# Output products that begin with branches A and B, a rounded copy of their own for the first block, and the gate stores moved to the front

## The chip, the core and the metric

The kernel runs on one core of one Trainium2 chip. The core has five engines that each work through their own queue of instructions: PE (TensorE, matrix products), DVE (VectorE), ACT (ScalarE), POOL (GpSimd) and SP (SyncE, which only issues transfers here). They meet through semaphores: an instruction can raise one when it ends, and a wait in an engine's queue holds everything behind it. The metric is the device time of one execution in microseconds (us), lower is better.

## What is computed

One layer of a hybrid backbone on 128 context tokens and 1024 latent tokens, width 1024, everything in fp32. Cut to what matters here:

```
h = rms_norm(x, g_pre) * (1 + scale) + shift
za, zb, zc, gc = split(h @ w_in)            # 1024 x 4096
ya = bg * conv_a(cg * xa) * silu(ga)        # branch A, 256 channels
u  = conv_b(u1 * sigmoid(u2)) + bias        # branch B: width 31 along grid columns
yb = silu(layer_norm(u)) * silu(gb)
yc = (group_norm(rwkv7 scans of zc) + bonus) * silu(gc)   # branch C, 512 channels
out = concatenate([ya, yb, yc]) @ w_out     # 1024 x 1024
x   = x + gate * rms_norm(out, g_post)
```

Every large product is made of three passes over rounded values: a number is split into a rounded part and the rest, and the product is rounded x rounded + rounded x rest + rest x rounded. So each factor needs two elementwise passes before its first product: the rounding (on ACT) and the subtraction that gives the rest (on POOL or DVE).

## The kernel before

The program has three parts with a barrier between them: the input projection with the convolutions (0 to 518 us of the trace), the scans of branch C (518 to 968 us), and the last part, group norm and output projection (968 to 1129 us). The change touches the first and the last.

**First part.** PE computes 32 tiles of 128 output channels, two for each of 16 pieces of `w_in`, in the order of `PIECES`: gc (4 tiles), u2 (2), u1 (2), gb (2), xa, cg, bg, ga (2 each), then 14 tiles for branch C. A tile has three column blocks, each of 24 matmuls, and takes three of six PSUM banks, so PE can start tile j only when some engine has read tile j-2 (`read_by`). DVE reads the gc, u1, gb, cg, bg and ga tiles, and in between does the width-31 convolution of branch B: 62 taps, two halves of 31. A tap is two instructions (L830), one for the context and one for the latent tokens, except the middle tap, which comes first in its half and is one (L823). The table `taps_after` says how many taps stand behind each of the tiles from the first u1 tile (number 6) to the last ga tile (17). The first tap also waits until both transfers that store the gate of branch C (`spill(4, ...)` and `spill(6, ...)`, L381, semaphore `s_sg`) have landed, since the convolution writes where the gate lay. SP issues these two among the loads of `w_in` and of the modulation weights. Those loads go round a ring of three buffers, and each waits until the buffer's content of three loads before has been used:

```
if (kind, k) == ("z", 4):
    spill(4, T[:, 4:6, :], s_gc, 2, s_sg)
if (kind, k) == ("z", 5):
    spill(6, T[:, 6:8, :], s_gc, 4, s_sg)
```

After the first C tile's first block PE also does the sums of branch B's layer norm (L645 to L654), which wait for the last tap.

**Last part.** The 1158 columns (tokens with their borders) are cut into three blocks of 388, 384 and 386. For each block there are four channel groups of branch C. `statistics(b)` on PE sums means, bonus and variances against DVE (L1882, L1885) and ACT (L1820); ACT takes the root (L1798), DVE inverts (L1890), PE spreads the result (`spreads(b)`, L1740), DVE normalises (L1895), ACT scales (L1803), POOL adds the bonus (L1871), DVE gates (L1901), ACT rounds (L1830) and DVE forms the rest (L1919). ACT also rounds the four parts of `w_out` (L1824), whose rests are formed by POOL (first part) and DVE (L1673, the other three), and block by block the branches A and B, called `yab` (L1834, rest on POOL, L1874). `output(i)` makes the 48 matmuls of token tile i, three tiles to a block: the 24 with branch C first, then the 24 with A and B. PE's order is statistics(0), spreads(0), output(0), statistics(1), output(1), spreads(1), output(2), statistics(2), output(3), spreads(2), output(4) to (8). For each tile `mean_square(i)` on ACT and `finish(i)` on DVE (L1907 to L1914) end the work; `finish(1)` stands in DVE's queue in front of the centring of block 2. The residual rows of x wait in three slots `xr`; tiles 0, 1 and 2 are loaded at once, later ones when their slot has been stored.

Of the kernel before, what the change touches and what calls it, by code (L numbers as in the profile page):

```python
# [30 lines left out]
P = 128  # L31
# [72 lines left out]
def hybrid_step_kernel(nc, x_prompt, x_sample, c, state_rwkv, c_ctx, ada_w, ada_b, g_pre, g_post, w_in,  # L104
# [3 lines left out]
    with ctx:  # L108
# [225 lines left out]
        with nc.Block() as block:  # L334
            @block.sync
            def _(sp):
# [46 lines left out]
                for n, (kind, k) in enumerate(LOADS):  # L383
                    if n >= RING:
                        before, m = LOADS[n - RING]
                        used, per = {"gate": (s_gu, 1), "z": (s_z, 2)}[before]
                        sp.wait_ge(used, per * (m + 1))
                    elif n:
                        sp.wait_ge(s_wu, 6 + n)
                    if kind == "gate":  # L390
                        sp.dma_start(ring[:, slot_of("gate", k), :].rearrange("p (k n) -> p k n", k=2),
                                     ada_w[0, 2 * k * P:2 * (k + 1) * P, 2048:3072].rearrange("(k p) n -> p k n", p=P)
                                     ).then_inc(s_wl[slot_of("gate", k)], 16)
                    elif k:
                        load_z(k)
                    if (kind, k) == ("z", GATE_AFTER + GATES + 2):
                        sp.wait_ge(s_gr, 1)
                        for s in range(2):
                            sp.dma_start(gate_dram[s:s + 1, :].rearrange("o (b n) -> (o b) n", n=256), grow[s:P:32, :]).then_inc(s_gst, 16)
                    if (kind, k) == ("z", 4):  # L400
                        spill(4, T[:, 4:6, :], s_gc, 2, s_sg)
                    if (kind, k) == ("z", 5):
                        spill(6, T[:, 6:8, :], s_gc, 4, s_sg)
                    if (kind, k) == ("z", MIX0 // 2 + RING):
                        spill(0, ya, s_ya, 2, s_sa)
                    if (kind, k) == ("z", MIX0 // 2 + RING + 1):
                        spill(2, T[:, 6:8, :], s_yb, 2, s_sb)
# [306 lines left out]
            def _(dve):  # L714
# [87 lines left out]
                taps_after = dict(zip(range(U1, MIX0), (5, 6, 6, 6, 7, 7, 3, 3, 6, 6, 4, 3)))  # L802
# [796 lines left out]
        BLOCK_W = max(b - a for a, b in zip(BLOCK_ENDS, BLOCK_ENDS[1:]))  # L1599
        take = carve()  # L1600
        take(8 * D_MODEL - 2 * W)
# [4 lines left out]
        XO = 3  # L1606
        xr = take(XO, D_MODEL)
# [68 lines left out]
        with nc.Block() as block:  # L1676
            @block.sync
            def _(sp):
# [9 lines left out]
                for c in range(WO_PARTS):  # L1688
                    at = 2 * P * WO_ORDER[c]
                    sp.dma_start(wo[:, wo_part(c), :],  # L1690
                                 w_out[0, at:at + 2 * P, :].rearrange("(k p) n -> p k n", p=P)).then_inc(s_wo[c], 16)
                load_gate(0)
                sp.dma_start(yab, mix_dram[0:4].rearrange("m p w -> p m w")).then_inc(s_ab, 16)
# [3 lines left out]
                for i in range(9):  # L1697
                    if i >= XO:
# [10 lines left out]
            def _(pe):  # L1709
# [43 lines left out]
                def output(i):  # L1753
                    pe.wait_ge(f_yl, needs[i])
# [3 lines left out]
                    for n in range(8):  # L1758
                        k = 2 * WO_ORDER[n // 2] + n % 2
                        if i == 0 and n % 2 == 0:  # L1760
                            by = REST_OF_WO_BY[n // 2]
                            pe.wait_ge(f_wr[by], REST_OF_WO_BY[:n // 2 + 1].count(by))
                        if n == 4:
                            pe.wait_ge(f_al, needs[i] // 4)
                        hi, rest = (yab_hi, yab_lo) if k < 4 else (y_hi, y_lo)
                        hi, rest = (v[:, k % 4, at:at + P] for v in (hi, rest))
                        for b in range(2):
                            o, cut = ps[:, 2 * (i % 2) + b, :], slice(512 * b, 512 * b + 512)
                            pe.matmul(o, hi, wo_hi[:, k, cut], start=(n == 0), stop=False)  # L1769
                            pe.matmul(o, hi, wo_lo[:, k, cut], start=False, stop=False)  # L1770
                            last = pe.matmul(o, rest, wo_hi[:, k, cut], start=False, stop=(n == 7))  # L1771
                    last.then_inc(s_o, 1)
# [3 lines left out]
                output(0)  # L1776
                statistics(1)
                output(1)
# [9 lines left out]
            def _(act):  # L1788
# [37 lines left out]
                def round_inputs(b):  # L1826
# [4 lines left out]
                    if b == 0:  # L1831
                        act.wait_ge(s_ab, 16)
                    act.wait_ge(f_bo, 4 * b + 4)
                    act.activation(yab_hi[:, :, cut], yab[:, :, cut], ACT.Copy).then_inc(f_ah, 1)  # L1834

                bonus_keys(0)
                for n in range(4):
                    square(n)
                    if n < 3:
                        bonus_keys(n + 1)  # L1840
                for b in range(NB):
                    deviation(b)
                    if b == 0:
                        for c in range(WO_PARTS - 1):
                            round_w_out(c)
# [3 lines left out]
                    if b == 0:  # L1849
                        round_w_out(WO_PARTS - 1)  # L1850
# [11 lines left out]
            def _(pool):  # L1862
# [4 lines left out]
                rest_of_w_out(pool, 0)  # L1867
                for n, (a, cut) in enumerate(BLOCKS):
# [3 lines left out]
                    if a == 3:  # L1872
# [5 lines left out]
            def _(dve):  # L1878
# [42 lines left out]
                for b in range(NB):  # L1921
# [9 lines left out]
                    invert(b)  # L1931
                    for n in group:
# [7 lines left out]
                    if b == 0:  # L1940
                        for c in range(1, WO_PARTS):
# [29 lines left out]
```

## Time and profile before

| | us |
|---|---|
| median of 3 runs (lowest to highest) | 1130.68 (1130.52 to 1131.49) |
| the profiled execution, its own time | 1131.15 |
| its span in the trace | 1129.3 |
| PE busy | 1018.8 (90% of the span) |
| DVE, ACT, POOL busy | 646.2, 426.8, 407.0 |
| granted TensorE clock, mean | 0.955 of full |

Busy shares are averages over three parts with different limits. What a change in one part is worth is read from that part: which wait ends last there. The profile's line of granted clock, in 40 slices of the span, stands at 9 tenths or more nearly everywhere, with a 7 in the second slice and 9, 6, 5 around the start of the scans:

```
PEclk9799998999899999996599999999999998989999
```

### The profile page before, as it was taken

The page shows a single profiled execution, that of the slowest core. Times are in us where ns is not written, and L with a number is a line of the kernel's source. Part 1 is how long each engine was busy: PE and PEld are TensorE (multiplying, and loading weights), DVE is VectorE, ACT ScalarE, POOL GpSimd, SP SyncE. Part 2 cuts the span into 40 slices and gives each one's busy share as a digit, 9 for nine tenths or more (in the row PEclk, how much of TensorE's full clock was granted, in tenths as well). Part 3 has the DMA queues.
Part 4 walks back from the last instruction along what each step waited for, and adds up shares of the span by engine and source line. Part 5 has one row for each costly group of instructions (what it writes and reads, how often), then busy time and mean ns, then how long its engine had stood idle before and what let it go on. Part 6 is the DMA issues. An engine that isn't in the chain of part 4 may idle for free. (4 is left out here: it accounts for less than half of the span.)

```text
span 1129.3 us, 32050 instructions
## 1 busy us (share of the span) xinstructions
PE 1018.8 (90%) x14407; PEld 916.6 (81%) x14407; DVE 646.2 (57%) x954; ACT 426.8 (38%) x708; POOL 407.0 (36%) x372
## 2 busy tenths in 40 slices
PE   5699998999789999994599999999999998779997
PEld 3399997999779988983599988999999997447685
DVE  5430019678564222243678878888888884365532
ACT  5351111101133333222355655566556552533311
POOL 7121220311104413321545545566666663232110
PEclk9799998999899999996599999999999998989999
DMA  9612332111102300000000000000000000641131
GB/s 360 239 38 75 117 117 75 38 38 38 38 3 86 108 6 32 1 1 10 1 3 4 4 13 4 4 4 4 4 3 5 3 4 3 242 170 48 64 112 56
DMA packets 30036, 61.46 MB, mean 54 GB/s; under 512 B 3352, under 2 KB 21444, under 8 KB 28748
## 3 DMA queue, kind: packets, MB, share of 16 engines
q1 hardware_dynamic: 29900, 59.42, 14.8%
q8 instruction: 114, 1.87, 0.7%
q14 instruction: 22, 0.18, 0.1%
HBM read 49.68 MB, written 9.73 MB: 53 GB/s over the span
## 5 line engine op out<-in xcount | busy, mean ns | idle before, releaser
L682 PE MATMUL ps<-input_rounded,weights_rounded 128*128 128x386 f32 x768 | 265.4, 346 | 10.6 <-DVE zc L888 6.0
L684 PE MATMUL ps<-input_rounded,weights_rest 128*128 128x386 f32 x768 | 261.4, 340 | 0.0
L683 PE MATMUL ps<-input_rest,weights_rounded 128*128 128x386 f32 x768 | 261.0, 340 | 0.0
L1403 POOL TENSOR_TENSOR arena<-arena,lvl 128x512 f32<-128x512 f32 x108 | 138.2, 1294 | 78.0 <-ACT arena L1320 46.8
L682 PEld LDWEIGHTS ps<-input_rounded,weights_rounded 128*128 128x128 f32 x768 | 146.1, 190 | 18.4 <-issue 9.3
L471 POOL TENSOR_TENSOR weights_rest<-arena,weights_rounded 128x2048 fp32r<-128x2048 f32 x16 | 75.3, 4707 | 218.9 <-ACT weights_rounded L516 218.9
L683 PEld LDWEIGHTS ps<-input_rest,weights_rounded 128*128 128x128 f32 x768 | 146.0, 190 | 0.7 <-issue 0.3
L684 PEld LDWEIGHTS ps<-input_rounded,weights_rest 128*128 128x128 f32 x768 | 146.0, 190 | 0.0
L1119 PE MATMUL ps<-arena 64*64 64x64 f32 x2880 | 107.7, 225 | 17.8 <-issue 14.6
L1119 PEld LDWEIGHTS ps<-arena 64*64 64x64 f32 x2880 | 95.8, 139 | 23.6 <-issue 17.1
L1129 PE MATMUL ps<-arena 64*64 64x64 f32 x2880 | 107.0, 226 | 4.4 <-DVE arena L1529 4.1
L1326 ACT ACTIVATE arena<-ps 128x512 f32<-128x512 f32 x90 | 53.8, 597 | 135.0 <-DVE arena L1533 127.0
L1129 PEld LDWEIGHTS ps<-arena 64*64 64x64 f32 x2880 | 95.0, 139 | 10.0 <-DVE arena L1529 5.9
L913 DVE SCALAR_TENSOR_TENSOR zc<-arena,hmu,zc 128x1156 f32<-128x1156 f32 x14 | 41.4, 2958 | 107.1 <-POOL arena L483 107.1
L483 POOL TENSOR_TENSOR arena<-arena 128x1156 f32<-128x1156 f32 x14 | 30.3, 2163 | 154.0 <-ACT arena L582 151.3
L1529 DVE TENSOR_TENSOR arena<-eyes,ps 128x512 f32<-128x512 f32 x90 | 61.4, 683 | 24.7 <-PE ps L1119 23.8
L830 DVE SCALAR_TENSOR_TENSOR zc<-zc,cb 128x113 f32<-128x113 f32 (+14 forms) x120 | 73.1, 651 | 1.9
L516 ACT ACTIVATE weights_rounded<-arena 128x2048 fp32r<-128x2048 f32 x16 | 30.6, 1915 | 98.6 <-DMA arena<-in_w_in 52.7
L1533 DVE STREAM_TRANSPOSE arena<-ps 128x512 f32<-128x512 f32 x72 | 51.2, 711 | 26.9 <-PE ps L1129 26.9
L581 ACT ACTIVATE zc<-ps,omu 128x1158 f32<-128x1158 f32 x14 | 17.2, 1227 | 110.8 <-PE ps L684 110.8
L1508 DVE TENSOR_TENSOR arena<-ps,tri 128x512 f32<-128x512 f32 x72 | 46.4, 686 | 16.7 <-PE ps L1099 16.7
L1099 PE MATMUL ps<-arena 64*128 64x128 f32 x576 | 44.2, 297 | 11.1 <-DVE arena L1500 11.1
(241 smaller groups left out, 1721.4 us busy)
## 6 DMA issues: line engine op xcount, KB each, us to landing
arena<-in_w_in SPq DMA_DIRECT2D x16, 1024.0 KB, 5.3
arena<-in_ada_w SPq DMA_DIRECT2D x7, 1024.0 KB, 5.2
mix_scratch<-zc SPq DMA_DIRECT2D x4, 1158.0 KB, 9.3
out<-arena SPq DMA_DIRECT2D x9, 512.0 KB, 2.6
zc<-in_x_sample SPq DMA_DIRECT2D x4, 1024.0 KB, 8.8
hT<-in_ada_w SPq DMA_DIRECT2D x4, 1024.0 KB, 12.0
zc<-in_w_out SPq DMA_DIRECT2D x4, 1024.0 KB, 8.2
arena<-in_x_sample SPq DMA_DIRECT2D x8, 512.0 KB, 3.5
```

Of the source, the lines that this page charges most:

```text
L471: pool.tensor_tensor(w_rest[:, at, :], ring[:, at, :], w_round[:, p % 2, :].bitcast(F32), ALU.subtract).then_inc(s_wo1, 1)
L682: pe.matmul(o, w_hi[:, k, cut], hi_of_h[:, k, cols_b], start=(k == 0), stop=False)
L683: pe.matmul(o, w_hi[:, k, cut], lo_of_h[k][:, cols_b], start=False, stop=False)
L684: last = pe.matmul(o, w_lo[:, k, cut], hi_of_h[:, k, cols_b], start=False, stop=(k == KT - 1))
L830: done = dve.scalar_tensor_tensor(out=o[:, a:b], in0=x[:, a + off * step:b + off * step], scalar=w, in1=o[:, a:b], op0=ALU.mult, op1=ALU.add)
L1119: last = pe.matmul(bank(0)[r, h, :], Um[l % 3][r, h, :], X[n % 2][r, h, :], start=True, stop=True)
L1129: last = pe.matmul(bank(1)[r, h, :], PX[r, h, :], Y[n % 2][r, h, :], start=True, stop=True)
L1326: act.activation(Y[n % 2], bank(1), ACT.Copy).then_inc(q_Y, 1)
L1403: pool.tensor_tensor(Um[l % 3], UT, lvl[:, l, :].unsqueeze(1).to_broadcast([P, 2 * PAIRS, C]), ALU.mult).then_inc(q_um[l], 1)
L1508: dve.tensor_tensor(GM[n % 2][:, d, h:h + PAIRS].rearrange("p a s c -> p a (s c)"), ps[:, 4 + 2 * d + g, :].rearrange("p (a k) -> p a k", ...
L1529: dve.tensor_tensor(PX, eye8(), bank(0), ALU.subtract).then_inc(q_F, 1)
L1533: dve.transpose(X[n % 2], bank(1)).then_inc(q_X, 1)
```

## The change

It has two halves.

In the first part both stores of the gate are issued behind the load of piece 3, and the taps are dealt out anew: more behind the early tiles, fewer behind the late ones.

```
@@ SP, first part
-if (kind, k) == ("z", 4):
+if (kind, k) == ("z", 3):
     spill(4, T[:, 4:6, :], s_gc, 2, s_sg)
-if (kind, k) == ("z", 5):
     spill(6, T[:, 6:8, :], s_gc, 4, s_sg)
@@ DVE, first part
-taps_after = dict(zip(range(U1, MIX0), (5, 6, 6, 6, 7, 7, 3, 3, 6, 6, 4, 3)))
+taps_after = dict(zip(range(U1, MIX0), (8, 8, 8, 8, 7, 7, 3, 3, 4, 3, 2, 1)))
```

In DVE's queue around the two u1 tiles (the 128x1158 rows of L888, in the change L887, read them; L830, in the change L829, are taps, the middle tap L823 stands ahead). Before:

```order
L830 SCALAR_TENSOR_TENSOR zc<-zc,cb 128x115
L830 SCALAR_TENSOR_TENSOR zc<-zc,cb 128x192
L830 SCALAR_TENSOR_TENSOR zc<-zc,cb 128x116
L830 SCALAR_TENSOR_TENSOR zc<-zc,cb 128x256
L888 SCALAR_TENSOR_TENSOR zc<-zc,ps 128x1158
L830 SCALAR_TENSOR_TENSOR zc<-zc,cb 128x117
L830 SCALAR_TENSOR_TENSOR zc<-zc,cb 128x320
```

and in the change:

```order
L829 SCALAR_TENSOR_TENSOR zc<-zc,cb 128x116
L829 SCALAR_TENSOR_TENSOR zc<-zc,cb 128x256
L829 SCALAR_TENSOR_TENSOR zc<-zc,cb 128x117
L829 SCALAR_TENSOR_TENSOR zc<-zc,cb 128x320
L829 SCALAR_TENSOR_TENSOR zc<-zc,cb 128x118
L829 SCALAR_TENSOR_TENSOR zc<-zc,cb 128x384
L829 SCALAR_TENSOR_TENSOR zc<-zc,cb 128x119
L829 SCALAR_TENSOR_TENSOR zc<-zc,cb 128x448
L887 SCALAR_TENSOR_TENSOR zc<-zc,ps 128x1158
```

Three more taps stand in front of the reading of the second u1 tile. At the other end of the table one tap, not three, stands behind the last ga tile.

In the last part the products of `output(i)` with A and B come first. For the first two tiles the halves are apart, and the queues are turned to suit: on SP the parts of `w_out` are loaded in the order 0 to 3 with `yab` behind the first; on ACT the first part is rounded among the squares of block 0, then `yab` of the first block into a buffer of its own, then the second part, and the last two at the end of the block; POOL forms the first rest of `yab` in front of its additions; DVE forms the rest of the second part of `w_out` between the inversion and the normalising of block 0. The new buffer lies over the second and third slot of `xr`, so the residual rows of tiles 1 and 2 are loaded only when output(2), the last tile that reads the buffer, is done.

```
-WO_ORDER = (2, 3, 0, 1)
+WO_ORDER = (0, 1, 2, 3)
+yab_first = rounded("branches_of_first_block_rounded", arena_at + 4 * (xr_from + D_MODEL), 4, BLOCK_ENDS[1])
@@ SP
 for i in range(9):
+    if i == 1:
+        sp.wait_ge(s_o, NB)
     if i >= XO:
         sp.wait_ge(s_st2[i % XO], 16 * (i // XO))
@@ PE
+def branch_products(i):
+    at = first_col[i]
+    if i >= 2:
+        pe.wait_ge(s_og, i - 1)
+    pe.wait_ge(f_al, needs[i] // 4)
+    whole = yab_hi if i >= NB else yab_first
+    products(i, 0, whole, yab_lo, at)
+def gated_products(i):
+    pe.wait_ge(f_yl, needs[i])
+    products(i, 4, y_hi, y_lo, first_col[i]).then_inc(s_o, 1)
 statistics(0)
 spreads(0)
-output(0)
+branch_products(0)
+branch_products(1)
+gated_products(0)
 statistics(1)
-output(1)
+gated_products(1)
 spreads(1)
@@ ACT
+    if n == 1:
+        round_w_out(0)              # among the squares of block 0
 deviation(b)
 if b == 0:
-    for c in range(WO_PARTS - 1):
-        round_w_out(c)
+    act.wait_ge(s_ab, 16)
+    act.activation(yab_first, yab[:, :, CUTS[0]], ACT.Copy).then_inc(f_ah, 1)
+    round_w_out(1)
...
 if b == 0:
-    round_w_out(WO_PARTS - 1)
+    round_w_out(2)
+    round_w_out(3)
@@ POOL, in front of the additions
+pool.wait_ge(f_ah, 1)
+pool.tensor_tensor(yab_lo[:, :, CUTS[0]], yab[:, :, CUTS[0]], yab_first.bitcast(F32),
+                   ALU.subtract).then_inc(f_al, 1)
@@ DVE
 invert(b)
+if b == 0:
+    rest_of_w_out(dve, 1)
```

DVE's queue in block 0 of the last part (L1890 and L1913 are the inversion, L1895 and L1918 the normalising, L1919 and L1942 the rest of branch C). Before:

```order
L1890 RECIPROCAL arena<-arena 128x388
L1895 TENSOR_TENSOR hT<-hT,ps 128x388 x3
L1901 SCALAR_TENSOR_TENSOR hT<-arena,hT 128x388
L1895 TENSOR_TENSOR hT<-hT,ps 128x388
L1901 SCALAR_TENSOR_TENSOR hT<-arena,hT 128x388 x3
L1919 TENSOR_TENSOR yc_rest<-hT,yc_rounded 128x388 x4
L1673 TENSOR_TENSOR w_out_rest<-zc,w_out_rounded 128x2048 x3
```

and in the change:

```order
L1913 RECIPROCAL arena<-arena 128x388
L1674 TENSOR_TENSOR w_out_rest<-zc,w_out_rounded 128x2048
L1918 TENSOR_TENSOR hT<-hT,ps 128x388 x3
L1924 SCALAR_TENSOR_TENSOR hT<-arena,hT 128x388
L1918 TENSOR_TENSOR hT<-hT,ps 128x388
L1924 SCALAR_TENSOR_TENSOR hT<-arena,hT 128x388 x3
L1942 TENSOR_TENSOR yc_rest<-hT,yc_rounded 128x388 x4
L1674 TENSOR_TENSOR w_out_rest<-zc,w_out_rounded 128x2048 x2
```

One subtraction over a part of `w_out` now stands in front of the whole chain of branch C.

SP's queue at the start of the last part (`zc<-in_w_out` are the parts of `w_out`, `zc<-mix_scratch` is `yab`, `arena<-mix_scratch` are gate blocks). Before:

```order
L1690 DMA zc<-in_w_out 128x2x1024 x4
L1686 DMA arena<-mix_scratch 128x4x388
L1693 DMA zc<-mix_scratch 128x4x1158
L1686 DMA arena<-mix_scratch 128x4x384
L1686 DMA arena<-mix_scratch 128x4x386
L1696 DMA arena<-gate_scratch 128x2048
```

and in the change:

```order
L1691 DMA zc<-in_w_out 128x2x1024
L1694 DMA zc<-mix_scratch 128x4x1158
L1691 DMA zc<-in_w_out 128x2x1024
L1687 DMA arena<-mix_scratch 128x4x388
L1691 DMA zc<-in_w_out 128x2x1024 x2
L1687 DMA arena<-mix_scratch 128x4x384
L1687 DMA arena<-mix_scratch 128x4x386
L1701 DMA arena<-gate_scratch 128x2048
```

`yab` is second in the queue, where it was sixth.

## Rows read from the trace of the kernel before

**Rows 1.** Waits of PE, 60 to 480 us: engine, line, releaser: total, times, longest.
```profile
PE ps L682 <- DVE zc L888: 6.0, 1, 6.0
PE ps L645 <- DVE zc L830: 5.9, 1, 5.9
```

**Rows 2.** Timeline of DVE from 60 us: start, duration, instruction [idle before <-releaser].
```profile
166.14 4.16 DVE L823 TENSOR_SCALAR zc<-zc,cb,vec 128x1158 f32<-128x1158 f32 x1 [22.83 <-DMA mix_scratch<-zc]
170.34 2.64 DVE L830 SCALAR_TENSOR_TENSOR zc<-zc,cb 128x113 f32<-128x113 f32 x8
```

**Rows 3.** Timeline of ACT: its first instruction on tiles 5, 8 and 9.
```profile
128.10 1.14 ACT L562 ACTIVATE zc<-ps 128x1158 f32<-128x1158 f32 x1 [11.54 <-PE ps L684]
168.47 1.14 ACT L566 ACTIVATE zc<-ps 128x1158 f32<-128x1158 f32 x1 [3.44 <-PE ps L684]
190.13 1.14 ACT L566 ACTIVATE zc<-ps 128x1158 f32<-128x1158 f32 x1 [20.52 <-PE ps L684]
```

**Rows 4.** Timeline of SP at piece 3's load, and the stores' transfers (KB, us to landing).
```profile
102.57 0.37 SPq L346 DMA_DIRECT2D arena<-in_w_in  x1
...
mix_scratch<-zc SPq DMA_DIRECT2D x4, 1158.0 KB, 9.3
```

**Rows 5.** Taps behind the last ga tile (ns min/median/max), and POOL beside them.
```profile
L830 DVE SCALAR_TENSOR_TENSOR zc<-zc,cb x6: 280/342/4573, 296.7 to 302.5; 128x115 f32<-128x115 f32 x1, 128x192 f32<-128x192 f32 x1, 128x114 f32<-128x114 f32 x1, 128x128 f32<-128x128 f32 x1
...
295.77 5.38 POOL L471 TENSOR_TENSOR weights_rest<-arena,weights_rounded 128x2048 fp32r<-128x2048 f32 x1 [21.22 <-ACT weights_rounded L516]
```

**Rows 6.** One us in PE's second wait: PE, PEld, DVE, ACT, POOL busy, clock, DMA.
```profile
300.00:301.00 1.00, 0.00 (x0) 0.00 (x0) 1.00 (x1) 0.00 (x0) 1.00 (x1) 0.50 0.00 0
```

**Rows 7.** Timeline of PE in the last part: spreads, outputs and statistics where they begin.
```profile
983.10 4.56 PE L1740 MATMUL ps<-arena 128*128 128x388 f32 x8 [3.76 <-DVE arena L1890]
994.28 0.79 PE L1769 MATMUL ps<-w_out_rounded,yc_rounded 128*128 128x512 f32 x1 [6.62 <-DVE yc_rest L1919]
...
1007.99 0.81 PE L1716 MATMUL ps<-hT,heads 128*128 128x384 f32 x2
...
1017.24 0.51 PE L1769 MATMUL ps<-w_out_rounded,yc_rounded 128*128 128x512 f32 x1
...
1028.52 3.07 PE L1740 MATMUL ps<-arena 128*128 128x384 f32 x8
...
1042.59 0.81 PE L1716 MATMUL ps<-hT,heads 128*128 128x386 f32 x2
```

**Rows 8.** Timeline of DVE in the last part.
```profile
984.77 0.56 DVE L1895 TENSOR_TENSOR hT<-hT,ps 128x388 f32<-128x388 f32 x1 [1.82 <-PE ps L1740]
...
1043.43 0.56 DVE L1882 SCALAR_TENSOR_TENSOR hT<-ps,hT 128x386 f32<-128x386 f32 x1 [0.44 <-PE ps L1716]
...
1053.93 1.23 DVE L1914 TENSOR_TENSOR arena<-arena 128x1024 f32<-128x1024 f32 x1
```

**Rows 9.** Transfers of the last part: first and last issue, landing times, KB.
```profile
L1690 SPq DMA_DIRECT2D zc<-in_w_out x4: 398/464/797, 969.8 to 971.3; - x4
...
DMA to landing us min/median/max: 5.0/8.2/11.3
...
zc<-mix_scratch SPq DMA_DIRECT2D x1, 2316.0 KB, 17.7
...
arena<-in_x_sample SPq DMA_DIRECT2D x8, 512.0 KB, 3.5
```

**Rows 10.** Roundings and rests, by line (ns min/median/max).
```profile
L1824 ACT ACTIVATE w_out_rounded<-zc x4: 1896/1899/1902, 980.2 to 994.2; 128x2048 fp32r<-128x2048 f32 x4
L1673 DVE TENSOR_TENSOR w_out_rest<-zc,w_out_rounded x3: 2280/2284/5603, 994.1 to 1001.9; 128x2048 fp32r<-128x2048 f32 x3
L1673 POOL TENSOR_TENSOR w_out_rest<-zc,w_out_rounded x1: 4541/4541/4541, 982.2 to 982.2; 128x2048 fp32r<-128x2048 f32 x1
L1834 ACT ACTIVATE branches_rounded<-zc x1: 1481/1481/1481, 992.8 to 992.8; 128x1552 fp32r<-128x1552 f32 x1
L1874 POOL TENSOR_TENSOR branches_rest<-zc,branches_rounded x3: 3527/3551/5439, 994.4 to 1073.0; 128x1552 fp32r<-128x1552 f32 x1, 128x1536 fp32r<-128x1536 f32 x1, 128x1544 fp32r<-128x1544 f32 x1
```

More of the change, by code:

```diff
@@ L1599, in hybrid_step_kernel @@
         BLOCK_W = max(b - a for a, b in zip(BLOCK_ENDS, BLOCK_ENDS[1:]))
+        XO = 3
         take = carve()
-        take(8 * D_MODEL - 2 * W)
+        xr_from = 8 * D_MODEL - 2 * W + 4
+        take(xr_from)
+        xr = take(XO, D_MODEL)
         gt = take(4, W)
@@ L1605, in hybrid_step_kernel @@
         back = take(4, P)
-        XO = 3
-        xr = take(XO, D_MODEL)
         gout = take(2, D_MODEL)
@@ L1686, in load_gate, with load_w_out @@
                     sp.dma_start(gt[:, :, cut], mix_dram[4:8, :, cut].rearrange("m p w -> p m w")).then_inc(s_gl[b], 16)
-                for c in range(WO_PARTS):
+                def load_w_out(c):
                     at = 2 * P * WO_ORDER[c]
@@ L1757, in output @@
                         pe.wait_ge(s_og, i - 1)
[L1758 to L1766, printed above, removed]
+                    pe.wait_ge(f_al, needs[i] // 4)
@@ new lines, in branch_products, with products @@
+                    whole = yab_hi if i >= NB else yab_first
[3 more added lines that the diff above has]
+                    products(i, 4, y_hi, y_lo, first_col[i]).then_inc(s_o, 1)
+                def products(i, k0, whole, rests, at):
+                    for k in range(k0, k0 + 4):
+                        if i == 0 and k % 2 == 0:
+                            by = REST_OF_WO_BY[k // 2]
+                            pe.wait_ge(f_wr[by], REST_OF_WO_BY[:k // 2 + 1].count(by))
+                        hi, rest = (v[:, k % 4, at:at + P] for v in (whole, rests))
@@ L1767, in output @@
                         for b in range(2):
                             o, cut = ps[:, 2 * (i % 2) + b, :], slice(512 * b, 512 * b + 512)
-                            pe.matmul(o, hi, wo_hi[:, k, cut], start=(n == 0), stop=False)
+                            pe.matmul(o, hi, wo_hi[:, k, cut], start=(k == 0), stop=False)
                             pe.matmul(o, hi, wo_lo[:, k, cut], start=False, stop=False)
-                            last = pe.matmul(o, rest, wo_hi[:, k, cut], start=False, stop=(n == 7))
@@ L1772, in output @@
-                    last.then_inc(s_o, 1)
+                            last = pe.matmul(o, rest, wo_hi[:, k, cut], start=False, stop=(k == 7))
+                    return last
+                def output(i):
+                    branch_products(i)
+                    gated_products(i)
                 statistics(0)
                 spreads(0)
-                output(0)
+                branch_products(0)
+                branch_products(1)
+                gated_products(0)
                 statistics(1)
-                output(1)
+                gated_products(1)
@@ L1830, in round_inputs @@
                         act.activation(y_hi[:, n % 4, cut], y[:, n % 4, cut], ACT.Copy).then_inc(f_yh, 1)
[L1831 to L1834, printed above, removed]
+                    if b:
+                        act.wait_ge(f_bo, 4 * b + 4)
+                        act.activation(yab_hi[:, :, cut], yab[:, :, cut], ACT.Copy).then_inc(f_ah, 1)
                 bonus_keys(0)
@@ L1940, in _ @@
                     if b == 0:
-                        for c in range(1, WO_PARTS):
+                        for c in range(2, WO_PARTS):
                             rest_of_w_out(dve, c)
```

10 lines of the change are left out of this document (6 added, 4 removed).

## Prediction

> **What bounds the kernel now.** I read the page first: PE is busy 90% of the span, so time can only come from where PE waits or runs at a low clock. The view of PE's waits comes next. In the first part it has two waits worth the name: 6.0 us for DVE's reading of the second u1 tile, and 5.9 us for the last tap of the convolution [rows 1]. Then the timelines, to see why. DVE stood idle for 22.83 us in front of the first tap, for a store of the gate [rows 2]; the second u1 tile's reading stands behind five taps in the same queue, and so came late. ACT's first touches of tiles 8 and 9 are 21.66 us apart where two tiles in step are 12.68 apart (11.54 idle + 1.14) [rows 3]: the 6.0 us of waiting cost 8.98 us in all, the other 3.0 being matmuls at the lower clock level. The second wait shows that fall too: the granted clock is 0.50, the 1.2 GHz level, 4 us after PE's last matmul there [rows 6].
>
> In the last part PE waits 3.76 us for the inversion and 6.62 us for the rest of branch C; from 994.28 on it never waits again, up to the tail [rows 7]. So there every us by which the outputs begin earlier is gained, and every us of a new wait is lost.
>
> **First part: stores and taps.** In the change both stores are issued behind the load of piece 3, which SP issued at 102.57; the second also needs the fourth gate tile, which PE ends about then too (128.10 less two tiles). With 9.3 us to land [rows 4], and the second queued behind the first, both are there by 123. The first u1 tile is ready at 128.10 + 12.68 + about 1 for the modulation products = 142, so the taps begin right behind it. Eight taps now stand in front of the second u1 tile's reading: the first five took 4.16 + 2.64 us (the 4.16 lengthened by POOL), three more at up to 1 us each (each longer than the 0.66 us of the pairs before): 7 to 10 us, against 12.68 for a tile. DVE is in time, and the first wait goes with its clock loss: **-9.0 us**. What is late next? Eight taps behind each later tile are at most 10 us, plus one hold of up to 4.6 us by POOL (below); PE needs a tile's reading only when it has made the next tile, so 14.6 and a reading stand against two tiles, 25.4. Nothing. The stores follow the load of piece 3 and cannot hold it up, and the load behind them waits for a tile that ends only at 128.
>
> The second wait is different. Behind the last ga tile stood three taps, six instructions. The first took 4573 ns where the median is 342, since POOL's subtraction ran from 295.77 to 301.15 [rows 5]. One tap instead of three takes away four short instructions, 4 x 0.3 = 1.2 us, and the instruction that is held stays: POOL's subtraction follows the same ACT rounding at the same distance. So the wait shrinks from 5.9 to about 4.7, **-1.2 us**. Bounds: 0, if the hold ends later, and -5.9, if POOL and the tap should miss each other. I take 1.2, by the row. The clock falls within 4 us of idleness there already, so I count no gain of clock. All later tiles of the part move with PE; the scans are untouched.
>
> **Last part: the early start.** I follow the changed queues. The first part of `w_out` lands at 969.8 + 5.0 = 974.8, the last of four at 971.3 + 11.3 = 982.6, so 2.6 us per 1024 KB [rows 9]. `yab`, now second, has 2316 KB: 5.9 us, so 980.7; the second part of `w_out` 983.3. ACT rounds `yab` of the first block (1.48 us) to 982.2 and the second part (1.9) to 985.2. POOL, done with part 0's rest by about 981.4 (974.8 + 1.9 + 4.54, with a little delay), forms the rest of `yab` from 982.2 to 985.8 (3.55; 5.44 where DVE was in its way) [rows 10]. DVE's new subtraction has two SBUF inputs and waits until POOL is done, like the held tap: 985.8 + 2.28 = 988.1. Only then does it normalise, at 988.1 instead of 984.77 [rows 8]. That holds PE: spread 2 needs normalising 0, so the last two spreads (4.56 / 4 = 1.14 each [rows 7]) run from 988.7 to 991.3 with the hand-overs. The branch products begin at 991.3 instead of 994.28: **-3.0 us**, not the 6 to 7 us that the wait offers. The rest of branch C then comes 3.3 us later than before, at 997.6, but is wanted only after 48 products: from 994.28 to 1007.99 these took 13.7 us, so at 1005; the last rests of `w_out` (2 x 2.28 behind it) are ready at 1002.2. Hidden, by 2.8 us. Bounds of this term: -5.2, if DVE's subtraction starts right after the inversion (rounding earlier than I have it), and -1.0, if POOL needs its longest 5.44.
>
> Forty-eight matmuls took 11.28 us at full clock (1017.24 to 1028.52), 13.7 after the wait, so the low level costs 2.4 us at the start, now as before.
>
> **Last part: what is covered less.** Between statistics(1) and spreads(1) stood output(1), 11.28 us; now 5.6. Root and inversion alone needed 3.76 in block 0, and finish(0) adds about 2.5 (twice 1.23), partly beside the root. **+0.3 us**, between 0 and 1.
>
> **Last part: the residual.** The rows of tile 1 are loaded only when output(2) is done, which ends at 1042.6 - 2.7 = 1039.9. The load takes 3.5 us [rows 9], the addition of finish(1) 1.23, hand-overs 0.1: DVE reaches the centring of block 2 at 1044.7. Before, it came 0.84 us after PE had begun statistics(2) (1043.43 - 1042.59) [rows 7, 8]; now it comes 4.8 us after. PE has only its first sums to do and then waits: **+4.0 us**, in a chain where nothing hides it. Bounds 3.5 and 5.5 (the load shares the queue with that of tile 2). The granted clock may fall in this wait, as it did within 4 us in rows 6: 0 to 3.0 us (the price at tile 9); I take **+1.5**. finish(2) and the later loads have many us to spare.
>
> **Sum.** -9.0 - 1.2 - 3.0 + 0.3 + 4.0 + 1.5 = -7.4 us. From the profiled execution's own 1131.15 us (span 1129.3 and 1.85 around it) that is 1123.75. This execution lay 0.47 above the median of 1130.68, so for a median: **1123.3 us**. First part -10.2, last part +2.8.
>
> **A rule weighed.** In the trace the transfers of one queue landed one after another, at 2.6 us per 1024 KB [rows 9], and the forecast rests on that order. The Trainium skill, "DMA: Bandwidth & Descriptors", in its section "Queues, rings and completion order", says that completion is not first in, first out for an issuing engine. If a later transfer could pass `yab`, the third rival below would be the likely case; by the rows it is not.
>
> **Rivals.**
>
> 1. The last part gains. The subtraction on DVE comes at 983.4, the branch products begin 5.2 us early and the clock stays up in the new wait. For it: POOL's rest of `yab` is the only thing between ACT's rounding and DVE, and whether the clock falls in a wait of 4 us is at the edge of what rows 6 show. Against: ACT must round `yab` and part 1 first. -10.2 - 5.2 + 0.3 + 4.0 = -11.1: 1119.6 us.
> 2. The first gain is partly lost again. The taps, brought forward, run into more of POOL's subtractions, DVE reads a later tile late, and a wait of one hold (4.6 us) returns. Against: a tile's reading has 24 us. -7.4 + 4.6 = -2.8: 1127.9 us.
> 3. Slower: `yab` lands as late as before. It was issued at about 972.7 and landed 17.7 us later, at 990.4. ACT's queue now waits for it in front of everything that block 0 still needs (part 1, the scaling of branch C), and so do DVE's subtraction and normalising. Each us after 980.7 costs one: 9.7 us, 1133.0 us. It decides from a landing at 988.1, where 7.4 us are used up. For it: it is the largest transfer of the part, and everything shares the one queue. Against: it stood sixth in the queue then, behind five transfers, and is second now.
> 4. The stores do not let the taps go earlier (the second held up behind the ring's waits). Then the 9.0 us stay: 1132.3 us. Against: the fourth gate tile is read three tiles ahead of the first tap.
>
> **How the numbers follow.** Forecast 0.70, rival 1 0.14, rival 2 0.08, rival 3 0.04, rival 4 0.01, and 0.03 for what I haven't seen, half of it within the bound. The forecast's own range, from its terms' bounds, is 1120.5 to 1126.5. For 8 in 10 I give 1119.5 to 1127.0, which takes in rival 1 and leaves rivals 2 to 4 out. About 0.2% (2.3 us) is what a measurement of this kernel can tell from no change. Forecast, rivals 1 and 2 are faster by more: 0.93; same 0.03; slower 0.04.
>
> **What would show it.** In the first part: the first tap near 143.5 with no wait for a store; tiles 8 and 9 12.7 us apart; PE's wait for the last tap near 4.7 us with one tap of about 4.6 in it. In the last part: DVE's subtraction over `w_out` ending near 988 (less 10 us of shift from the first part), the first product with A and B 3 us earlier than the first output did, PE at work from there to output(2)'s end but for a few tenths, then a wait of about 4 us on PE in statistics(2), with DVE's addition in finish(1) waiting for a load. I am wrong if PE waits in front of the branch products beyond 994 (in the old numbering), if statistics(2) has no wait, or if tile 9 still comes late.

## The result: 1118.9 us, below the predicted range

| | before | after |
|---|---|---|
| median of the runs, us | 1130.6 (1130.49 to 1131.49, 4 runs) | 1118.88 (1118.71 to 1119.15, 4 runs) |
| profiled execution, us | 1131.15 | 1118.77 |
| its span, us; mean granted clock | 1129.3; 0.955 | 1117.1; 0.961 |

The ratio is 0.9896, with a 95% interval of 0.988 to 0.9912: 11.7 us faster, where 7.4 were forecast. Over more executions of both kernels the difference is 10.1 on average; why single comparisons differ so much is the main finding below.

**The first part.** The waits of PE from 60 to 480 us in the changed kernel (columns as in [rows 1]); the wait for the second u1 tile is not in the list any more:

```profile
PE ps L644 <- DVE zc L829: 4.6, 1, 4.6
```

DVE's timeline at the first taps, against [rows 2] (142.14 is the reading of the first u1 tile, 143.54 the first tap):

```profile
142.14 1.36 DVE L887 SCALAR_TENSOR_TENSOR zc<-zc,ps 128x1158 f32<-128x1158 f32 x1 [37.78 <-PE ps L683]
143.54 0.88 DVE L822 TENSOR_SCALAR zc<-zc,cb,vec 128x1158 f32<-128x1158 f32 x1
144.46 1.87 DVE L829 SCALAR_TENSOR_TENSOR zc<-zc,cb 128x113 f32<-128x113 f32 x6
```

The taps begin right behind the first u1 tile's reading, with no wait for a store, and ACT's first touches of tiles 8 and 9 are 12.68 us apart, against 21.66 in [rows 3]:

```profile
168.66 1.14 ACT L565 ACTIVATE zc<-ps 128x1158 f32<-128x1158 f32 x1 [4.25 <-PE ps L683]
181.34 1.14 ACT L565 ACTIVATE zc<-ps 128x1158 f32<-128x1158 f32 x1 [11.54 <-PE ps L683]
```

The sums of the layer norm begin at 292.73, where they began at 302.87. The tap behind the last ga tile, which they wait for, is still held:

```profile
287.91 4.77 DVE L829 SCALAR_TENSOR_TENSOR zc<-zc,cb 128x113 f32<-128x113 f32 x2
292.73 1.66 PE L644 MATMUL ps<-zc,arena 128*128 128x386 f32 x2 [4.58 <-DVE zc L829]
```

**The last part.** PE's timeline, against [rows 7]. Each row is one place: spreads 0 and 1, spreads 2 and 3, first branch product, statistics(1), spreads(1), statistics(2), its continuation behind the wait, output(3):

```profile
970.28 2.92 PE L1747 MATMUL ps<-arena 128*128 128x388 f32 x4 [3.68 <-DVE arena L1913]
975.28 2.92 PE L1747 MATMUL ps<-arena 128*128 128x388 f32 x4 [2.08 <-DVE hT L1918]
977.43 1.21 PE L1780 MATMUL ps<-w_out_rounded,s_of_first_block_rounded 128*128 128x512 f32 x1
...
995.45 0.81 PE L1723 MATMUL ps<-hT,heads 128*128 128x384 f32 x2
...
1010.63 3.15 PE L1747 MATMUL ps<-arena 128*128 128x384 f32 x8
...
1024.80 0.81 PE L1723 MATMUL ps<-hT,heads 128*128 128x386 f32 x2
...
1030.72 1.55 PE L1723 MATMUL ps<-hT,heads 128*128 128x386 f32 x2 [4.46 <-DVE hT L1905]
...
1039.77 0.50 PE L1780 MATMUL ps<-w_out_rounded,branches_rounded 128*128 128x512 f32 x1
```

DVE's timeline at the same two places, against [rows 8]:

```profile
972.26 2.41 DVE L1674 TENSOR_TENSOR w_out_rest<-zc,w_out_rounded 128x2048 fp32r<-128x2048 f32 x1 [2.12 <-ACT w_out_rounded L1841]
974.59 1.01 DVE L1918 TENSOR_TENSOR hT<-hT,ps 128x388 f32<-128x388 f32 x2
...
1028.97 1.22 DVE L1937 TENSOR_TENSOR arena<-arena 128x1024 f32<-128x1024 f32 x1 [5.64 <-DMA arena<-in_x_sample]
```

SP's issue of that load, and the first matmul of output(3) in the kernel before, which [rows 7] do not reach:

```profile
1024.99 0.81 SPq L1707 DMA_DIRECT2D arena<-in_x_sample  x2
```

```profile
1051.87 0.50 PE L1769 MATMUL ps<-w_out_rounded,yc_rounded 128*128 128x512 f32 x1
```

The part began at 957.05 (first matmul with `heads`), after 969.86. Counted from there, the spreads begin at 13.2 as before, the subtraction over `w_out` ends at 17.6, the branch products begin at 20.4 (the first output stood at 24.4), and statistics(2) begins at 67.8, before at 72.7. There the new wait stands: DVE is held by a load that SP issued only at 1024.99, PE waits 4.46 us, and the pair of matmuls behind the wait takes 1.55 us where it took 0.81. From statistics(2) to output(3) it is 15.0 us, before 9.2 (1042.59 less 969.86 is 72.7, output(3) began at 82.0). The whole part is 160.05 us, before 159.44.

**Where the time went.** From the timelines, stage by stage, with the profiled executions of all later runs, since one pair turned out to mislead. A: start to ACT's touch of tile 5. B: to the layer norm's first sum. C: to SP's first load of the scans. D: to the last part. E: to the end of the span.

| kernel | A | B | C | D | E |
|---|---|---|---|---|---|
| before | 128.1 | 174.8 | 213.2 | 453.8 | 159.4 |
| r_before, the same again | 128.7 | 174.4 | 213.0 | 450.4 | 159.4 |
| e2_last | 128.3 | 174.3 | 212.9 | 453.4 | 159.8 |
| e4_taps | 128.3 | 176.1 | 214.7 | 451.4 | 160.2 |
| e3_stores | 128.1 | 165.8 | 214.7 | 453.5 | 159.5 |
| e1_first | 127.0 | 164.4 | 214.7 | 448.4 | 159.1 |
| after | 128.3 | 164.4 | 214.7 | 449.6 | 160.1 |
| r_after, the same again | 127.8 | 164.4 | 212.8 | 453.4 | 160.2 |
| e5_noresid | 127.9 | 164.4 | 212.9 | 453.5 | 154.4 |
| e7_pool | 128.3 | 164.4 | 212.8 | 453.6 | 158.9 |
| e8_both | 127.8 | 164.4 | 214.6 | 448.8 | 152.2 |
| e6_fill | 127.4 | 164.4 | 214.6 | 456.8 | 158.5 |
| e9_fill6 | 128.4 | 164.4 | 212.8 | 451.6 | 152.7 |

B and E answer to the edits. C and D hold code that no edit but the fillers touches, and yet they move: C by 1.9, D by up to 5.3 us without fillers, and by 1.9 and 3.8 between two executions of the changed kernel. A moves by 1.7 us, and no edit explains that either. In the seven profiles with the earlier stores and no fillers, all three with a short C have a long D, and three of the four with a long C have a short D (e3_stores is the exception). So the draws of C and D may hang together, which was not followed up.

### The profile page after: what moved, and what is told of

It reads as the page before. It is cut to its first block and busy times, and to the rows that moved or that the text cites. A ratio compares the mean times of both kernels' runs of the same rounds, so it can differ in the third digit from the quotient of the medians.

```text
span 1117.1 us, 32049 instructions
## 1 busy us (share of the span) xinstructions
PE 1013.8 (91%) x14407; PEld 910.3 (81%) x14407; DVE 643.6 (58%) x954; ACT 427.3 (38%) x708; POOL 404.3 (36%) x372
## 5 line engine op out<-in xcount | busy, mean ns | idle before, releaser
L1118 PE MATMUL ps<-arena 64*64 64x64 f32 x2880 | 106.0, 224 | 18.2 <-issue 14.7
L1118 PEld LDWEIGHTS ps<-arena 64*64 64x64 f32 x2880 | 94.5, 137 | 23.8 <-issue 17.0
L1128 PE MATMUL ps<-arena 64*64 64x64 f32 x2880 | 104.9, 223 | 4.5 <-DVE arena L1528 4.1
L1128 PEld LDWEIGHTS ps<-arena 64*64 64x64 f32 x2880 | 92.9, 137 | 10.2 <-DVE arena L1528 6.1
L829 DVE SCALAR_TENSOR_TENSOR zc<-zc,cb 128x113 f32<-128x113 f32 (+14 forms) x120 | 77.4, 687 | 1.8
```

The costliest lines, as they stand in the source:

```text
L829: done = dve.scalar_tensor_tensor(out=o[:, a:b], in0=x[:, a + off * step:b + off * step], scalar=w, in1=o[:, a:b], op0=ALU.mult, op1=ALU.add)
L1118: last = pe.matmul(bank(0)[r, h, :], Um[l % 3][r, h, :], X[n % 2][r, h, :], start=True, stop=True)
L1128: last = pe.matmul(bank(1)[r, h, :], PX[r, h, :], Y[n % 2][r, h, :], start=True, stop=True)
```

## The experiments

**Each half alone.** e1_first is the kernel before with the two edits of the first part (`("z", 3)` and the new `taps_after`); e2_last has all the others.

> The kernel before with the first part of the change alone (both gate stores behind piece 3's load, new table of taps). Theory A (the last scan step's clock depends on when it comes, after 9 us less work ahead of it): layer-norm sums 10.1 us earlier, mix tiles 8.6 earlier, last part begins 12.8 earlier with no low clock in the last scan step; in all -12.8, 1118.3 us. Rival B (the scans' gain comes from something in the last part's edit, such as where buffers lie): the last part begins 9.0 us earlier, the low clock in the last scan step is still there; -9.0, 1121.7 us.

Measured: 1121.02 us median, 1115.53 to 1122.06 in 5 runs, ratio 0.9921 (0.9894 to 0.9948). The layer norm's sums come 10 us earlier, as expected (B). But the profiled execution ran at 1115.53 and the four others at 1119.95 to 1122.06: neither theory had single executions of one kernel 6.5 us apart. The profiled one began its last part 15.3 us earlier than before and had the clock up in the last scan step, as theory A says; the median lies near theory B's 1121.7. The run alone decides for neither.

> The kernel before with the last part of the change alone (order of loads, branch products first, own rounded copy, residual loads held). Theory A: up to the last part nothing moves, the low clock stays in the last scan step (957.0 less 969.86 doesn't happen), and the last part takes 0.6 us more: 1131.3 us. Rival B: the last part begins 3.8 us earlier, 1127.5 us.

Measured: 1129.73 us median, 1126.04 to 1132.02 in 10 runs, ratio 1.0001 (0.9985 to 1.0017). Up to the last part nothing moves, and the last part takes 0.3 us more (159.75 against 159.44). The last part's edits are worth nothing by themselves: what the early products give, the residual's wait takes.

**Stores and taps apart.** e3_stores:

```diff
-                    if (kind, k) == ("z", 4):
+                    if (kind, k) == ("z", 3):
                         spill(4, T[:, 4:6, :], s_gc, 2, s_sg)
-                    if (kind, k) == ("z", 5):
                         spill(6, T[:, 6:8, :], s_gc, 4, s_sg)
```

e4_taps: `(5, 6, 6, 6, 7, 7, 3, 3, 6, 6, 4, 3)` becomes `(8, 8, 8, 8, 7, 7, 3, 3, 4, 3, 2, 1)`, with the stores where they were.

> The kernel before with only the two gate stores issued at piece 3, old table of taps. If the stores alone held the first tap, the 6.0 us wait for the second u1 tile goes (tile 9 12.7 us behind tile 8, -9.0), and the 5.9 us wait for the last tap stays. The last scan step then lies 9 us earlier, close to where the whole change has it: 1118.5 to 1119.5 if its clock stays up, 1121.7 to 1123 if it falls. If the table is needed too, 1129 or more.

> The kernel before with only the new table of taps, stores in their old place. Eight taps instead of five stand in front of the second u1 tile's reading, still behind the late store: the 6.0 us wait grows by three taps of 0.66 to 0.8 us, 8.0 to 8.4 us; the last tap's wait shrinks from 5.9 to 4.6. In all +0.8 to +1.2 without the clock: 1131.7 us; 1 to 4 us more or less if the clock's falls (at tile 9, in the last scan step) change with it.

e3_stores: 1118.34 us median (1118.12 to 1123.32, 4 runs), ratio 0.9918 (0.9885 to 0.9951). The stores alone take the first wait away (B 165.8, so -8.5 to -9.0) and leave the second as it was. The table adds 1.34 us to that: 164.44 in e1_first against 165.78. The profiled execution, with the clock down in the last scan step, is the one of 1123.32 us; the three others lie between 1118.12 and 1118.49. e4_taps: 1131.86 us (10 runs), ratio 1.0023 (1.0005 to 1.004). PE's waits of e3_stores, then of e4_taps:

```profile
PE ps L644 <- DVE zc L829: 5.9, 1, 5.9
```

```profile
PE ps L682 <- DVE zc L888: 8.8, 1, 8.8
PE ps L645 <- DVE zc L830: 4.6, 1, 4.6
```

The new table without the earlier stores makes the first wait longer, 8.8 us (8.0 to 8.4 expected), since eight taps instead of five stand behind the late store in front of the second u1 tile's reading. B grows by 1.4 to 1.9 us, the median by 2.3. So the new table needs the earlier stores, the stores do not need the table, and only the stores bring much.

**The same kernels again.**

> The changed kernel once more, word for word. Theory A now (the low clock in the last scan step comes in some executions of any of these kernels and not in others; the change takes only 9 us off): single executions between 1115.5 and 1122 as with the first part alone, with steps of 1 to 4 us between them, and the mean near before less 9. Rival B (the change does away with that low clock): every execution within 1118.5 to 1119.5, as in the first four, 11 to 12 us under before.

> The kernel before once more, word for word. If low clock in the last scan step is a matter of the single execution: times from 1125.5 to 1131.6, and, if this profiled execution is one of the faster ones, a last scan step as in the changed kernel's first profile (scans 449.6 us instead of 453.8). If it belongs to the program: 453.8 again.

r_after: 1119.18 us median, 1116.64 to 1121.15 in 6 runs, ratio 0.9907 (0.989 to 0.9925). r_before: 1128.18 us median, 1125.45 to 1133.39 in 10 runs, ratio 0.9999. Theory A as told for r_after holds: its executions spread over 4.5 us, which the four of the first comparison, within 0.5 us of each other, did not show. PE's timeline in the last full scan step of the kernel before, in its first profile:

```profile
949.39 1.15 PE L1129 MATMUL ps<-arena 64*64 64x64 f32 x32 [0.79 <-DVE arena L1529]
951.40 1.61 PE L1119 MATMUL ps<-arena 64*64 64x64 f32 x32 [0.87 <-issue]
953.79 1.97 PE L1129 MATMUL ps<-arena 64*64 64x64 f32 x32 [0.78 <-DVE arena L1529]
```

and in r_before, word for word the same program:

```profile
949.74 1.15 PE L1129 MATMUL ps<-arena 64*64 64x64 f32 x32 [0.79 <-DVE arena L1529]
951.75 1.15 PE L1119 MATMUL ps<-arena 64*64 64x64 f32 x32 [0.86 <-issue]
953.68 1.15 PE L1129 MATMUL ps<-arena 64*64 64x64 f32 x32 [0.78 <-DVE arena L1529]
```

Up to 951 the two go in step 0.35 us apart, with the same waits of 0.8 to 0.9 us between products and updates. Then the same 32 matmuls take 1.97 us in the one and 1.15 in the other. The stretch around it, as windows of 12 us that begin near the same work and not at the same instruction (length; busy us of PE, PEld, DVE, ACT, POOL; granted clock; DMA), of before, r_before, after and r_after in turn:

```profile
950.00:962.00 12.00, 9.49 (x204) 9.03 (x200) 3.47 (x6) 1.19 (x2) 0.00 (x0) 0.58 0.01 3
```

```profile
947.00:959.00 12.00, 8.70 (x286) 8.13 (x282) 5.29 (x9) 1.91 (x4) 2.27 (x2) 1.00 0.02 5
```

```profile
937.00:949.00 12.00, 8.70 (x280) 8.07 (x277) 5.45 (x9) 1.79 (x3) 2.27 (x2) 1.00 0.02 4
```

```profile
938.00:950.00 12.00, 9.49 (x198) 9.03 (x199) 3.47 (x6) 1.19 (x2) 0.60 (x1) 0.59 0.01 3
```

Each kernel has an execution with the clock down and one with the clock up. The layer norm shows the same with its waits of about 1 and 2 us: windows of after, then of r_after, same columns:

```profile
316.00:320.00 4.00, 2.58 (x5) 1.49 (x5) 0.48 (x1) 0.85 (x1) 0.00 (x0) 0.68 0.00 0
```

```profile
316.00:320.00 4.00, 3.71 (x18) 3.18 (x19) 1.50 (x1) 2.10 (x3) 0.00 (x0) 1.00 0.00 0
```

That fall makes about 1.3 of the 1.9 us in column C. The other 0.6 come directly behind the wait for the last tap: 15.7 us after the layer norm's first sum the changed kernel is where r_after is after 15.1. So the 4.2 us by which D fell between the first two profiles (453.8 to 449.6) need no edit to explain them. What decides it in one execution, no run here shows. The Trainium skill, "TensorE: Matmul & The Clock Gate", in its section "Part 1: The HAM clock gate", says that the chip's look at PE's activity runs freely and does not start anew with a kernel; executions that part in the middle of equal work agree with that.

**Fillers in the scans.** e6_fill and e9_fill6 (the latter on top of e8_both) put unread matmuls behind the products and updates of the last full step, at seven places (the expectations say eight; the last product and update share one):

```diff
+                def keep_busy(n):
+                    if n == N - 1:
+                        pe.wait_ge(q_kv, 2 * N)
+                        for _ in range(16):                  # 6 in e9_fill6
+                            pe.matmul(ps[0:64, 4, 0:64], eyes[lo, :], eyes[lo, :], start=True, stop=True)
...
                         product(n2, 2)
+                        keep_busy(n2)
```

> The changed kernel with matmuls that nobody reads (8 x 16 of 64 columns, one operand, into a free bank) in PE's waits between products and updates of the last full scan step. If the low clock there comes from PE's idle share: no low clock in the last scan step, single executions lie closer together, near the fastest of the changed kernel (1115.5 to 1119). If it comes from something else, the spread and the low clock stay; fillers that reach beyond the waits cost up to 8 x 0.3 = 2.4 us.

> The kernel of e8_both with 6 unread matmuls, not 16, at each of the eight places (0.7 us each, which fits into waits of 0.8 to 0.9). If PE's idle share lets the clock fall in the last scan step: no low clock there at almost no cost, executions 0 to 4 us faster than e8_both, mean 1 to 2.5 us under it. If six are too few to hold it: the same spread as e8_both and up to 2 us slower, where a place has no wait to hide them.

e6_fill: 1125.24 us median (1123.54 to 1127.41, 11 runs), 6 us slower than r_after. The row of the fillers and the product's beside it:

```profile
941.60 1.97 PE L1219 MATMUL ps<-eyes 64*64 64x64 f32 x31
...
946.26 1.10 PE L1118 MATMUL ps<-arena 64*64 64x64 f32 x31
```

I had priced them by the product's 1.15 us per group, but those alternate between two halves of the array; sixteen fillers took 1.97 us, more than a wait is long. The fillers also all write one place, so which of the two makes them slower was not separated. e9_fill6: 1111.67 us (1111.31 to 1112.83, 4 runs), 2.2 us slower than e8_both and so just outside what was expected. One window of each:

```profile
938.00:958.00 20.00, 20.00 (x521) 19.86 (x520) 5.25 (x9) 2.96 (x6) 2.28 (x2) 1.00 0.02 4
```

```profile
936.00:950.00 14.00, 13.44 (x386) 12.82 (x383) 5.45 (x9) 2.15 (x4) 2.27 (x2) 1.00 0.02 5
```

With PE full the clock was up in both profiles. Of the eleven without fillers it was down in six (before, e2_last, e3_stores, r_after, e5_noresid, e7_pool), down for part of the stretch in one (e4_taps) and up in four (r_before, after, e1_first, e8_both). That fits the theory, but two profiles do not prove it. The expectation also had the executions closer together, and that failed: those of e6_fill spread over 3.9 us, hardly less than r_after's 4.5. So this stretch is not shown to be what makes the spread; C and A move too. As a remedy it failed: six fillers cost 2.9 us in D (451.6 against 448.8 in e8_both), and the low clock, which comes only in some executions, 3.4 us in the kernel before (453.8 less 450.4).

**The residual's wait.** e5_noresid gives the rounded copy a place of its own, moves two small tiles into a hole behind `w_out`, and takes away what made SP wait:

```diff
-        sd = take(BLOCK_W)
-        back = take(4, P)
+        sd = zflat[:, 4 * W + 8 * D_MODEL:4 * W + 8 * D_MODEL + BLOCK_W]
+        back = zflat[:, 4 * W + 8 * D_MODEL + BLOCK_W:...].rearrange("p (a c) -> p a c", a=4)
...
-        yab_first = rounded(..., arena_at + 4 * (xr_from + D_MODEL), 4, BLOCK_ENDS[1])
+        yab_first = rounded(..., arena_at + 4 * first_at, 4, BLOCK_ENDS[1])    # behind all others
...
-                    if i == 1:
-                        sp.wait_ge(s_o, NB)
```

> The changed kernel with the rounded copy of the first block in a place of its own (deviation and spread matrix moved into a hole behind w_out), and no wait of SP for output(2) in front of the residual loads. If the wait of 4.5 us in statistics(2) and the low clock behind it are the price of the shared place: no wait of PE there, statistics(2) 9.2 us instead of 15, in all -4.5 to -6 against the changed kernel. If the loads, issued early again, hold up the other transfers, the branch products begin later and part of it is lost.

Measured: 1114.85 us median (1113.38 to 1115.33, 5 runs), ratio 0.9865 (0.9846 to 0.9884), 4.3 us under r_after by the medians and 4.7 by the means. PE and then DVE in statistics(2):

```profile
1026.52 0.81 PE L1723 MATMUL ps<-hT,heads 128*128 128x386 f32 x2
1027.16 0.81 PE L1727 MATMUL ps<-hT,heads 128*128 128x386 f32 x2
...
1035.81 0.50 PE L1780 MATMUL ps<-w_out_rounded,branches_rounded 128*128 128x512 f32 x1
```

```profile
1025.14 1.79 DVE L1937 TENSOR_TENSOR arena<-arena 128x1024 f32<-128x1024 f32 x1
1027.37 0.56 DVE L1905 SCALAR_TENSOR_TENSOR hT<-ps,hT 128x386 f32<-128x386 f32 x1 [0.44 <-PE ps L1723]
```

DVE's addition follows its predecessor without a wait, and statistics(2) is back at 9.3 us (1026.52 to 1035.81). The part is 154.4 us, 5.7 less than the changed kernel's. The branch products still begin at 20.4: the early loads stood behind all others in the queue and held nothing up.

**DVE's subtraction.** e7_pool is the changed kernel with `REST_OF_WO_BY = (0, 0, 1, 1)`, `rest_of_w_out(pool, 1)` behind the branches' rest, and without `rest_of_w_out(dve, 1)` in front of the normalising.

> The changed kernel with the second part of w_out's rest formed by POOL (behind the branches' rest) and not by DVE in front of the normalising. If DVE's subtraction is what holds spreads 2 and 3 (wait of 2.1 us) and so the branch products: that wait goes, the branch products begin at stage 17 instead of 20.4 (-3 to -3.9 us), and the gated products still find branch C ready. If POOL, held up by 4.5 us, brings the bonus sums late, a wait appears in front of the gated products and eats it: 0.

Measured: 1118.58 us median (1115.33 to 1121.57, 6 runs), ratio 0.9901 (0.988 to 0.9922), by the median not to be told from r_after. The profile shows more. PE, then POOL:

```profile
972.33 5.51 PE L1747 MATMUL ps<-arena 128*128 128x388 f32 x8 [3.63 <-DVE arena L1914]
977.06 1.21 PE L1780 MATMUL ps<-w_out_rounded,s_of_first_block_rounded 128*128 128x512 f32 x1
...
1030.36 1.65 PE L1723 MATMUL ps<-hT,heads 128*128 128x386 f32 x2 [4.39 <-DVE hT L1906]
1031.81 1.49 PE L1727 MATMUL ps<-hT,heads 128*128 128x386 f32 x2
```

```profile
971.41 3.20 POOL L1889 TENSOR_TENSOR branches_rest<-zc,s_of_first_block_rounded 128x1552 fp32r<-128x1552 f32 x1 [0.77 <-ACT s_of_first_block_rounded L1863]
974.56 4.55 POOL L1674 TENSOR_TENSOR w_out_rest<-zc,w_out_rounded 128x2048 fp32r<-128x2048 f32 x1
```

The eight spreads are one run, and the branch products begin at 18.0 of the part instead of 20.4. That is 2.4 us and not the 3 to 3.9 I expected, because the wait that goes was 2.1. In statistics(2) half of it is lost again: 16.1 us instead of 15.0, with the clock low for longer behind the residual's wait.

**Both.**

> The kernel of e5_noresid and e7_pool together: rounded copy in its own place with early residual loads, and the second part of w_out's rest on POOL. If both effects stand by themselves: branch products at 18.0 of the last part (20.4), no wait in statistics(2), last part 160.1 - 5.6 - 2.4 = 152 us, and the time 7 to 8 us under the changed kernel's 1119.1: 1111 to 1112.5. If the later bonus sums of POOL matter once the outputs follow each other without a wait: a wait shows in front of gated products, 1113 or more.

Measured: 1109.46 us median (1108.89 to 1109.94, 4 runs), ratio to before 0.9829 (0.9806 to 0.9851). The last part is 152.2 us, as the sum of the two said, with one wait of PE left behind the branch products' start:

```profile
PE ps L1780 <- DVE w_out_rest L1676: 0.8, 1, 0.8
```

This beats both kernels, and lies below the 1111 to 1112.5 expected. 7.9 us of its lead of 9.7 over r_after (160.1 less 152.2) are the two edits'. The clock in D was up in its profile; that this makes the rest in all four executions is not shown.

## Why the prediction was partly wrong

**What bounds the kernel, and the first part's mechanism: right.** The u1 wait went whole with its clock loss (-8.98 us between tiles 8 and 9, forecast -9.0), the taps began at 143.54 (near 143.5), the held tap stayed (4.77 us for two taps) and its wait shrank by 1.3 (forecast 1.2). B fell by 9.9 to 10.3 us, forecast 10.2.

**"The scans are untouched": the step that failed, as a reading of one profile.** Their code is untouched, but I took the one execution that [rows 1 to 10] come from as what the kernel always does. It had the clock down in the last scan step, and I didn't look there. Of the 12.2 us between the two spans, 2.7 are C and D (+1.5 and -4.2), and they are the draw of single executions. Over the profiles with this program before the last part and no fillers, C and D together average 665.4 us with the first part's edits (7 profiles) and 665.6 without (before, r_before, e2_last). So no shift of the scans by the edits shows, though with so few profiles one of 2 us could hide. But a forecast of a single comparison needed a term for the draw, and my range of 1119.5 to 1127.0 had none: executions of the kernel before lie up to 4 us on either side of their mean.

**The last part: right in what happens, 2.2 us off in size.** Forecast +2.8; the first pair of profiles has +0.6, and e2_last +0.3. Over all executions this is the larger error, since the draw mostly evens out there: 2.1 us (+0.7 instead of +2.8) of the 2.7 by which -7.4 misses -10.1.
- The early start was 4.0 us, not 3.0 (5.2 in e2_last, where the last four spreads took 1.62 us at full clock and not 2.92). DVE's subtraction began when ACT's rounding of the second part ended, at 15.2 of the part, and ended at 17.6, where I had it wait for POOL and end at 18.2 (988.1 less 969.86; rows below); the first product overlaps the last two spreads: it stands 2.76 us behind the end of the subtraction, where I had 3.2.

```profile
970.32 1.91 ACT L1841 ACTIVATE w_out_rounded<-zc 128x2048 fp32r<-128x2048 f32 x1 [1.07 <-DMA zc<-in_w_out]
969.32 3.20 POOL L1889 TENSOR_TENSOR branches_rest<-zc,s_of_first_block_rounded 128x1552 fp32r<-128x1552 f32 x1 [0.77 <-ACT s_of_first_block_rounded L1863]
```

- "The low level costs 2.4 us at the start, now as before" was wrong. The granted clock, windows at the branch products:

```profile
977.00:980.00 3.00, 3.00 (x8) 1.98 (x8) 3.00 (x5) 1.85 (x4) 2.31 (x3) 0.56 1.06 375
980.00:984.00 4.00, 4.00 (x19) 3.25 (x18) 3.48 (x7) 3.27 (x5) 0.68 (x1) 1.00 1.04 410
```

  It is at full from about 980, after 2.5 us of products; the 72 matmuls took 18.0 us (977.43 to 995.45) against 16.9 at full clock (72/48 of 11.28), 1.1 lost instead of 2.4. The repeats agree: 18.1 us in r_after, and for the 48 matmuls of the old order 13.6 in r_before. The wait ahead of them was 2.08 us and no longer 6.62; that this is why less was lost is argued, not tested, and e7_pool, with no wait there at all, lost as much (18.2 us).
- spreads(1) comes as little later as forecast (+0.3), and the residual's price was right: 4.0 + 1.5 forecast, 5.8 by the stage (15.0 less 9.2), 5.7 by e5_noresid.

**The rivals.** Rival 1 was half right: the subtraction's record begins 0.3 us before POOL was done (972.26 against 972.52) and is 0.13 us longer than the 2.28 of [rows 10], so whether it was held for that instant can't be told. ACT's rounding ended only 0.3 us before POOL, so little was gained by it; and the clock did fall in the new wait. Rival 2 didn't come: the first part has no new wait. Rival 3 didn't: `yab` was rounded from 967.75 on, 10.7 of the part, where I had 10.8, and the second part of `w_out` landed behind it (ACT's rounding of it begins at 970.32), in the order of issue. Rival 4 didn't: no tap waited for a store.

**The range.** My 1120.5 to 1126.5 was said to come from the terms' bounds. Those bounds, added up from 1130.68, give 1114.1 to 1130.2: the lower one has the -5.9 of the last tap's wait in it. So the range was narrower than its own terms, and no working of mine says why.

**Right and wrong in sum.** Forecast -7.4. The stages that belong to the edits give -10.05 + 0.75 = -9.3 (B's mean, and E's over after and r_after against before and r_before). All executions give 1119.0 (10 runs, standard deviation 1.2) against 1129.1 (59 of the later runs of before): -10.1, and the interval of r_after alone is -12.4 to -8.5. The 0.8 between -9.3 and -10.1 is within what the clock's draws leave open.

## What to carry to other kernels

A profile is one execution: look for stretches where PE's work is full of short waits, since there the clock may fall in one execution and not in the next, and give a forecast from a single pair a term for it. A buffer placed over another's slots is paid for by whoever waits for those slots; price that wait where nothing hides it, because here it took all that the early products gave. When a stall is removed by an early transfer, ask first which of the edits needs which: the stores alone brought about 9 of the first part's 10 us, the new order of taps alone cost about 2.

## What the runs showed of the hardware

- In the last scan step the granted clock fell to the 1.2 GHz level where PE's longest wait before the fall was 0.9 us (0.79 and 0.87 in the profile of before), and in other executions of the same program it did not. It cost 3.4 us in the kernel before and 3.8 in the changed one (column D, down less up).
- Groups of 32 recorded 64-column matmuls took 1.15 us where they alternate between two halves of the array, and about 2 us at full clock (31 of them 1.97) where all go to one half and write one place.
- Executions of one kernel lay between 1125.5 and 1133.4 us, and the mean granted clock tends to fall as they get longer: 0.961 at 1125.45, 0.954 at 1133.39, though single ones stand out (0.961 at 1128.63). The first four runs of before (1130.49 to 1131.49) showed nothing of that width.
